# High weights against both parts of x in one matmul, on the first four ways up

## The reference

```python
DEPTH, D_MODEL, D_FF, SEQ = 2, 1024, 2816, 256

def swiglu(x, w_gate_up, w_down):
    gate, up = jnp.split(x @ w_gate_up, 2, axis=-1)
    return (jax.nn.silu(gate) * up) @ w_down

for l in range(DEPTH):
    x = x + 0.5 * swiglu(rms_norm(x, ffn1_norm[l]), ffn1_w_gate_up[l], ffn1_w_down[l])
    ...                       # three sequence mixers between w_in and w_out
    x = x + 0.5 * swiglu(rms_norm(x, ffn2_norm[l]), ffn2_w_gate_up[l], ffn2_w_down[l])
```

## Time and profile before

| | |
|---|---|
| median of 3 runs | 1797.14 us (1796.92 to 1803.63) |
| profiled execution, its time | 1798.5 us |
| its span, from the first instruction to the last | 1796.5 us |
| mean granted TensorE clock | 0.984 of full speed |
| TensorE matmuls busy | 1725.7 us (96%) |
| VectorE busy | 1256.6 us (70%) |
| ScalarE busy | 889.7 us (50%) |
| POOL busy | 369.0 us (21%) |
| mean HBM traffic | 156 GB/s |

### The profile page before, as it was taken

The page is one execution under the profiler, slowest core; times in us unless marked ns, Lnnn a source line. Parts: engine busy times, 40 slices in busy tenths (PEclk is TensorE's granted clock), DMA queues, the critical chain, the costliest instruction groups (busy, mean ns, idle before and its releaser), DMA issues.

```text
span 1796.5 us, 35508 instructions
## 1 busy us (share of the span) xinstructions
PE 1725.7 (96%) x15248; PEld 1611.8 (90%) x15248; DVE 1256.6 (70%) x2101; ACT 889.7 (50%) x1566; POOL 369.0 (21%) x316
## 2 busy tenths in 40 slices
PE   7999999999899999999999999989999999979997
PEld 6999988887799998999998888779999888879987
DVE  5876675856667776677676576566787665789974
ACT  5664435323445654566443533344565555556652
POOL 3552000000212651156200000021265200121110
PEclk9999999999899999999999999989999999989999
DMA  8655522211146565565552221114556552335442
GB/s 301 238 222 194 213 94 94 75 46 49 49 162 258 214 233 185 212 252 211 194 215 92 94 95 34 40 48 166 222 210 234 188 192 104 118 141 181 174 151 104
DMA packets 44492, 282.86 MB, mean 157 GB/s; under 512 B 6064, under 2 KB 6704, under 8 KB 17712
## 3 DMA queue, kind: packets, MB, share of 16 engines
q1 hardware_dynamic: 44336, 280.60, 42.7%
HBM read 279.53 MB, written 1.05 MB: 156 GB/s over the span
## 4 chain that ended last, share of the span: by engine, by line
PE 83%; DVE 11%; ACT 3%; issue 1%; DMA 1%; POOL 0%; SPq 0%; DVEq 0%; ACTq 0%
PE bank L489 16%; PE bank L491 15%; PE bank L490 15%; PE bank L497 10%; PE bank L985 8%; PE bank L498 5%; PE bank L1581 4%; DVE WL L480 2%; ACT WH L475 2%; PE bank L1848 1%; PE bank L1125 1%; DVE XC L1054 1%; DMA ring<-wst 1%; PE bank L527 1%; PE bank L1858 0%
## 5 line engine op out<-in xcount | busy, mean ns | idle before, releaser
L489 PE MATMUL bank<-XNH,WH 128*128 128x256 f32 (+1 forms) x2176 | 620.7, 285 | 17.9 <-DVE XNL L573 12.3
L480 DVE TENSOR_TENSOR WL<-ring,WH 128x2048 fp32r<-128x2048 f32 (+1 forms) x235 | 509.4, 2170 | 162.9 <-ACT WH L475 162.7
L491 PE MATMUL bank<-XNH,WL 128*128 128x256 f32 (+1 forms) x2176 | 616.6, 283 | 0.0
L490 PE MATMUL bank<-XNL,WH 128*128 128x256 f32 (+1 forms) x2176 | 614.5, 282 | 0.0
L475 ACT ACTIVATE WH<-ring 128x2048 fp32r<-128x2048 f32 (+1 forms) x235 | 405.5, 1729 | 211.4 <-PE bank L491 133.1
L489 PEld LDWEIGHTS bank<-XNH,WH 128*128 128x128 f32 x2176 | 412.9, 190 | 23.6 <-DVE XNL L573 12.3
L490 PEld LDWEIGHTS bank<-XNL,WH 128*128 128x128 f32 x2176 | 414.3, 190 | 0.0
L491 PEld LDWEIGHTS bank<-XNH,WL 128*128 128x128 f32 x2176 | 414.1, 190 | 0.0
L497 PE MATMUL bank<-HP,WH 128*128 128x512 f32 x770 | 267.6, 392 | 0.8 <-POOL HP L882 0.7
L498 PE MATMUL bank<-HP,WL 128*128 128x256 f32 x770 | 215.5, 280 | 0.0
L985 PE MATMUL bank<-XN,ring 128*128 128x256 f32 x832 | 200.1, 389 | 0.0
(11 more groups left out here) (476 smaller groups left out, 2612.4 us busy)
## 6 DMA issues: line engine op xcount, KB each, us to landing
ring<-wst SPq DMA_DIRECT2D x206, 1024.0 KB, 4.8
ring<-wst SPq DMA_DIRECT2D x80, 704.0 KB, 4.2
LP<-lp SPq DMA_DIRECT2D x1, 1872.0 KB, 7.1
LP<-lp SPq DMA_DIRECT2D x1, 1792.0 KB, 8.4
X<-xin SPq DMA_DIRECT2D x2, 512.0 KB, 4.7
out<-X SPq DMA_DIRECT2D x4, 256.0 KB, 2.5
C<-cst SPq DMA_DIRECT2D x1, 193.0 KB, 10.7
AL<-cst SPq DMA_DIRECT2D x1, 192.0 KB, 10.6
```

Source lines behind the costliest of these rows:

```text
L480: e.do.tensor_tensor(WL[:, slot[q], 0:n], ring[:, i % NSLOT, 0:n], WH[:, slot[q], 0:n].bitcast(F32), ALU.subtract).then_inc(*w_dve.up("low ...
L489: e.do.matmul(o, WH[:, s, cols], xh, start=first, stop=False)
L490: e.do.matmul(o, WH[:, s, cols], xl, start=False, stop=False)
L491: return e.do.matmul(o, WL[:, s, cols], xh, start=False, stop=last)
```

## The change

For f = 0 to 3, step j calls `wide` 16 times and not `three`: 512 columns with WH and both parts of x, 256 columns with WL and the high part. XNH and XNL become the two halves of one tensor XNP, so that one access pattern reads both. The gate features get one bank and the up features another: step j owns the pair that begins at `first_bank(j)` = 2((j+1) % 3), so three steps are in PSUM where six were. The banks become one PSUM tensor `banks`, so that one instruction can read from two banks. TT2 and HT become the two halves of one tensor G2.

To add the halves: ScalarE copies the right halves of both banks to G2 (`act_half`, 512 columns), as the first thing in its step, after a wait for the matmuls of step j and for `hl` of step j-3; VectorE adds the left halves to it (`dve_added`), as the first thing in its step, and that frees the banks; `dve_taken` then multiplies the 512 columns of G2 by ACC in one instruction, ahead of `dve_low`. TensorE's step j waits for `added` of step j-3. For f = 4 nothing changes.

```diff
-        bank = [ctx.enter_context(nc.psum_tensor(f"bank{i}", [128, 512], F32)) for i in range(8)]
+        banks = ctx.enter_context(nc.psum_tensor("banks", [128, 8, 512], F32))
+        bank = [banks[:, i, :] for i in range(8)]
...
+        def first_bank(j):
+            return 2 * ((j + 1) % 3)
...
-                if j >= 6:
-                    e.wait_ge(*(f_act.on("taken", f, j - 6) if f == 4 else f_dve.on("taken", f, j - 6)))
+                if f == 4:
+                    e.wait_ge(*(f_act.on("taken", f, j - 6) if j >= 6 else b_dve.on("add", j)))
+                elif j >= 3:
+                    e.wait_ge(*f_dve.on("added", f, j - 3))
                 elif f in (1, 3):
-                    e.wait_ge(*o_dve.on("add", f // 2, j))
+                    e.wait_ge(*o_dve.on("add", f // 2, first_bank(j) + 1))
                 elif f == 2:
-                    e.wait_ge(*f_dve.on("add", f - 1, j))
+                    e.wait_ge(*f_dve.on("add", f - 1, first_bank(j) + 1))
...
-                        m = three(e, b[:, h * T:h * T + T], q, slice(at, at + 128), XNH[:, k, 0:T], XNL[:, k, 0:T], k == 0, k == KT - 1)
+                        if f < 4:
+                            m = wide(e, bank[first_bank(j) + h], q, slice(at, at + 128), XNP[:, :, k, 0:T], k == 0, k == KT - 1)
...
@@ act_ffn
             for j in range(NF):
+                if f < 4:
+                    act_half(e, f, j)
                 act_high(e, turn_of(gu, l, ("pair", j)) + AHEAD)
...
-        def dve_taken(e, f, j):
-            g, hs, b = TT2[:, j % 3, :], HT[:, j % 3, :], bank[j % 6]
+        def pair_halves(j, half):
+            return banks[:, first_bank(j):first_bank(j) + 2, T * half:T * half + T]
+
+        def act_half(e, f, j):
             e.wait_ge(*f_pe.on("gu", f, j))
-            e.wait_ge(*f_act.on("rstd", f))
             if j >= 3:
                 e.wait_ge(*f_pool.on("hl", f, j - 3))
-            e.do.tensor_tensor(g, b[:, 0:T], ACC[:, :], ALU.mult).then_inc(*f_dve.up())
-            e.do.tensor_tensor(hs, b[:, T:2 * T], ACC[:, :], ALU.mult).then_inc(*f_dve.up("taken", f, j))
+            e.do.activation(G2[:, j % 3, :, :], pair_halves(j, 1), ACT.Copy).then_inc(*f_act.up("half", f, j))
+
+        def dve_added(e, f, j):
+            e.wait_ge(*f_act.on("half", f, j))
+            e.do.tensor_tensor(G2[:, j % 3, :, :], pair_halves(j, 0), G2[:, j % 3, :, :], ALU.add).then_inc(*f_dve.up("added", f, j))
+
+        def dve_taken(e, f, j):
+            e.wait_ge(*f_act.on("rstd", f))
+            e.wait_ge(*f_dve.on("added", f, j))
+            e.do.tensor_tensor(G2[:, j % 3, :, :], G2[:, j % 3, :, :], ACC[:, :].unsqueeze(1).to_broadcast([128, 2, T]), ALU.mult).then_inc(
+                *f_dve.up("taken", f, j))
...
@@ dve_ffn
             for j in range(NF):
+                if f < 4:
+                    dve_added(e, f, j)
+                    if j == root_at(f):
+                        e.wait_ge(*f_pe.on("sums", f))
+                        dve_rsqrt(e, f_dve, bank[6][:, 0:2], 2, 1.0 / D, EPS, 0, ("rstd", f))
+                    if j > root_at(f) + 1:
+                        dve_taken(e, f, j)
                 dve_low(e, turn_of(gu, l, ("pair", j)) + AHEAD)
...
```

More of the change, by code:

```diff
@@ L330, in hybrid_kernel @@
         BEGINS = sb("BEGINS", [128, T])
-        TT2 = sb("TT2", [128, 3, T])
+        G2 = sb("G2", [128, 3, 2, T])
         SM = sb("SM", [128, 336])
@@ L375, in hybrid_kernel @@
             WL = sf("WL", [128, AHEAD, SLOT], F32R)
-            XNH = sf("XNH", [128, KT, T + 2], F32R)
-            XNL = sf("XNL", [128, KT, T + 2], F32R)
+            XNP = sf("XNP", [128, 2, KT, T + 2], F32R)
             with ExitStack() as part_c:
-                HT = part_c.enter_context(nc.sbuf_tensor("HT", [128, 3, T], F32))
                 GT = part_c.enter_context(nc.sbuf_tensor("GT", [128, 2, T], F32))
@@ L407, in hybrid_kernel @@
         X2 = XN
+        TT2, HT = G2[:, :, 0, :], G2[:, :, 1, :]
         HH, HL = HP[:, :, 0, :], HP[:, :, 1, :]
+        XNH, XNL = XNP[:, 0, :, :], XNP[:, 1, :, :]
         own = SM[:, 172:186]
@@ L496, in wide @@
             s = slot[q]
-            e.do.matmul(b[:, :], WH[:, s, cols], x.rearrange("p s t -> p (s t)"), start=first, stop=False)
+            e.do.matmul(b[:, :].rearrange("p (s t) -> p s t", s=2), WH[:, s, cols], x, start=first, stop=False)
             return e.do.matmul(b[:, 0:T], WL[:, s, cols], x[:, 0, :], start=False, stop=last)
@@ L628, in pe_ffn @@
                     e.wait_ge(*low_on(q))
-                if j >= 6:
-                    e.wait_ge(*(f_act.on("taken", f, j - 6) if f == 4 else f_dve.on("taken", f, j - 6)))
+                if f == 4:
+                    e.wait_ge(*(f_act.on("taken", f, j - 6) if j >= 6 else b_dve.on("add", j)))
+                elif j >= 3:
+                    e.wait_ge(*f_dve.on("added", f, j - 3))
                 elif f in (1, 3):
-                    e.wait_ge(*o_dve.on("add", f // 2, j))
+                    e.wait_ge(*o_dve.on("add", f // 2, first_bank(j) + 1))
                 elif f == 2:
-                    e.wait_ge(*f_dve.on("add", f - 1, j))
-                elif f == 4:
-                    e.wait_ge(*b_dve.on("add", j))
+                    e.wait_ge(*f_dve.on("add", f - 1, first_bank(j) + 1))
                 for h in range(2):
@@ L643, in pe_ffn @@
                         at = k * 256 + h * 128
-                        m = three(e, b[:, h * T:h * T + T], q, slice(at, at + 128), XNH[:, k, 0:T], XNL[:, k, 0:T], k == 0, k == KT - 1)
+                        if f < 4:
+                            m = wide(e, bank[first_bank(j) + h], q, slice(at, at + 128), XNP[:, :, k, 0:T], k == 0, k == KT - 1)
+                        else:
+                            m = three(e, b[:, h * T:h * T + T], q, slice(at, at + 128), XNH[:, k, 0:T], XNL[:, k, 0:T], k == 0, k == KT - 1)
                 m.then_inc(*f_pe.up("gu", f, j))
@@ L663, in pe_ffn @@
                 if n < 6:
-                    e.wait_ge(*(f_act.on("taken", f, last) if f == 4 else f_dve.on("taken", f, last)))
+                    e.wait_ge(*(f_act.on("taken", f, last) if f == 4 else f_dve.on("added", f, (20, 21, 19)[n // 2])))
                 elif n == 7 and f < 4:
@@ L840, in dve_ffn @@
                     dve_condition(e)
[L841 to L845, removed]
+                if f < 4 and j <= root_at(f):
                     continue
                 if f < 4 and j == root_at(f) + 1:
-                    for i in range(j):
+                    for i in range(j + 1):
                         dve_taken(e, f, i)
-                        if i:
+                        if 0 < i < j:
                             dve_gated(e, f, i - 1)
-                if f < 4:
-                    dve_taken(e, f, j)
-                else:
+                if f == 4:
                     dve_conv(e, j)
```

## The result

The changed kernel takes 1902.81 us (median of 4, 1897.0 to 1903.32) against 1798.18 for the kernel before measured beside it: a ratio of 1.0571, 95% interval 1.0558 to 1.0584. The prediction was 1905 us, 1865 to 1940. The profiled execution's span is 1901.1 us against 1796.5, 104.6 us more.

What follows compares the result with a forecast made beforehand. TensorE was taken to bound the kernel in the up phases. Per phase 26.3 us lost, 3.4 gained, 4 lost at the end: +26.9, four phases +107.6; 1798.5 + 107.6 - 1.4 = 1904.7, so 1905 us, range 1865 to 1940.

Steps and rivals of the forecast that it cites:

- The bound before: In the up phases TensorE sets the pace, busy 148.00 of 148 us; VectorE and ScalarE have slack.
- The wait that moved: Waiting for POOL's `hl(j-3)` moves from VectorE to ScalarE's `act_half`, closing a loop; each of five ada blocks costs 5.3 us.
- The loop's sizes: ScalarE-POOL loop: ordinary step 5.41 us, ada step 11.6, cycle 22.4 against 17.16 of TensorE.
- The contention in it: In ordinary steps, VectorE's low and POOL's `hl` share SBUF ports; `hl` takes 2.27 us instead of 0.74.
- Added, taken and half: New instructions per up step: `dve_added` and `dve_taken` 0.60 us each on VectorE, hidden beside high; `act_half` 0.54 on ScalarE.
- TensorE's saving: Up phases: pair of matmuls 346.4 ns against the triple's 356.1; 0.155 us a step, 13.7 us in all.
- The stalls' number and size: TensorE waits for low weights at j = 9, 12, 15, 18 and 21 of each up phase, about 5.3 us each.
- What a phase lost: Each up phase: 26.3 us lost in five stalls, 3.4 gained by the matmul pair, before the loss at its end.
- The end of a phase: First down tile after each up phase: TensorE waits for the last `hl`, losing 4 us or so.
- Rival A: Up phases: `hl` comes in time, TensorE stays the bound, only the 13.7 us saving remains: 1784 us; chance 5%.
- B: Up phases: the loop without contention, ordinary step 3.9 us, ada step 11.3, cycle 19.1: 1826 us; chance 8%.
- C: Up phases: VectorE becomes the bound and the loop doesn't, about 17.3 to 18.9 us a cycle: 1800 to 1835 us; chance 4%.

## Why the prediction was right

**The bound before** (TensorE, with the slack of the others) was right, and that slack wasn't the question: the wait's place was.

**The wait that moved** was the step that made the sign. The run with the wait alone shows it by itself (+56 us), and the one with four buffers removes it.

**The loop's sizes.** Ordinary step 5.41, measured 5.40 and 5.41; ada step 11.6, measured 11.50; cycle 22.4, measured 22.31. The contention in it (2.88 us from low's start to `hl`'s end) was taken from one row and held; the run with low behind gated shows its cause.

**Added, taken and half.** Added and taken take 0.69 us each where 0.60 was forecast; they hide beside high, as said. The copy is 0.60 us long and 0.49 to 0.50 from its start to that of the next, where 0.54 was forecast; 0.09 us from `hl`'s end to the copy, where 0.04 was, makes up for that. (By the prediction's own terms VectorE gets 1.20 - 0.84 = 0.36 us a step more and not the 0.6 it states; it got 1.38 - 0.84 = 0.54. Neither enters the sum.)

**TensorE's saving was mis-sized.** The pair's 346.4 ns came from the ways down, with another operand; on the ways up it is 351. 13.7 us were 7, or 1.9 us a phase and not 3.4.

**The stalls' number and size.** Five a phase at about 5.3 us were predicted, at steps 9, 12, 15, 18 and 21. They came at just these steps, but 21 of 3.0 us in the mean. The difference is the granted clock after them, which the prediction described and put outside the sum, as it fills the stall within a cycle.

**What a phase lost.** The prediction had 26.3 - 3.4 = 22.9 us, and it was 24.8 in the mean. The smaller saving is 1.5 us of the gap. Step 21 is 2.3 us: it took 8.10 (from the row at 162.62), 8.25, 7.28 and 8.30 us and not 5.7, as its matmuls ran at the lower clock behind the last stall; the prediction named this surcharge ("perhaps 2 us a phase") and left it out. The other way go the first stall of a phase, 4.05 to 4.80 us for 5.3, and the loop's surplus over TensorE's own cycle, 22.31 - 17.30 = 5.0 us for 5.24.

**The end of a phase was mis-sized.** 4 us a phase were predicted; 5.3 us in all lie outside the four phases, 4.3 of them in the ways down, 1.1 each. The slow step 21 is part of the reason: the first down tile comes later and meets `hl` sooner. In the third phase, where step 21 took 7.28 us, the way down lost 1.75 us, and in the others 0.76 to 0.95. In the run with the wait alone it lost 1.6 us where step 21 took 5.79 us, and 0.1 or less where it took 7.2 to 7.3. Even with the 2.3 us of step 21 added, the end of a phase cost 3.4 us and not 4.

So the mechanism was right and most terms were within a few per cent, but two terms missed by 2 to 3 us a phase in opposite directions, and that the sum, +107.6 against +104.6, is better than its parts is luck. Rival A fails by its own condition (the ada step would have to take under 6.3 us), B by the 2.23 us of `hl`, and C because VectorE is idle ahead of `added`, 82 us in all. The Trainium skill (VectorE: DVE Perf Modes, the section on the TRN2 errata) gives a matmul 6 + columns cycles, which would make the pair 325 ns, as an estimate; 346.4 to 351 were measured, and the measurement decides.

## What to carry to other kernels

When an edit moves a wait, look at what is queued behind it on that engine, and whether the thing waited for depends on that same engine's previous step; then follow one cycle instruction by instruction and add up the loop. If it is longer than the bound engine's cycle, the difference is paid every time, whatever the busy shares say. Before giving up such a change, try the order of the queue and one more buffer: here the same work went from +5.7% to -0.1% that way, and to -0.4% with rows of 272 columns.

## What the runs showed of the hardware that was not expected

- The pitch of one and the same pair of float32r matmuls (512 and 256 columns) depends on the operand's layout: 346.4 ns for the hidden layer's adjacent parts, 351.5 with rows of 1032 bytes, 348.2 to 349.5 with rows of 1088 bytes, 350.0 with rows of 1088 bytes and the parts next to one another.
- A short stall is enough to bring TensorE's clock down to the 1.2 GHz level. After the 2.25 us that end at 95.70 in the changed kernel, the stretch from 96 to 100 us shows a granted clock of 0.57, with pairs of 0.64 us. In the run with the wait alone, the clock is at 0.50 from 111.2 to 114.5 us, after a stall of 1.48 us that ends at 110.00. In both, four matmuls of a single column stand right before the stall. It isn't always so: of that run's eight stalls of 1.44 to 1.50 us, seven have such a slow stretch right behind them, and the one that ends at 670.9 has none.
- Contention for SBUF between VectorE and POOL isn't the same for every pair of instructions. `hl` takes 2.23 us beside a low of 2.29 us and 0.74 without. The three additions take 4.15 to 4.17 us in 22 of the changed kernel's 24 ada blocks, while the two VectorE operations beside them are stretched to 1.31 and 1.40 us, from 0.42 and 0.43 elsewhere. What these two cost POOL isn't shown, since no addition ran without one beside it.
